# Unrolled head pairs in MLA, maxima finished in PSUM, and a new order within an attention step

## The reference

```python
for i in range(DEPTH):                       # kinds 0, 1, 2, 0
    hc = mod_norm(xc, norm_g[i], sh_c, sc_c) # 256 context rows
    hl = mod_norm(xl, norm_g[i], sh_l, sc_l) # 1024 latent rows
    ...                                      # q, k, v by projection, rotary on the latents
    s = q @ k.T * scale                      # latents: 512 cached + 1024 own keys; context: its 256 own
    p = softmax(s)                           # SWA: band mask, and a sink logit in the denominator
    o = p @ v
    x = x + gate * ((o * silu(g)) @ w_out[i])
```

## Time and profile before

| | us |
|---|---|
| median of 3 runs | 3929.22 (3926.41 to 3936.61) |
| the profiled execution, its own time | 3931.54 |
| its span | 3929.7 |
| PE busy | 3555.3 (90%) |
| DVE busy | 2518.0 (64%) |
| ACT busy | 2168.8 (55%) |
| POOL busy | 1187.7 (30%) |

### The profile page before, as it was taken

The page is one execution under the profiler, slowest core; times in us unless marked ns, Lnnn a source line. Parts: engine busy times, 40 slices in busy tenths (PEclk is TensorE's granted clock), DMA queues, the critical chain, the costliest instruction groups (busy, mean ns, idle before and its releaser), DMA issues. The chain is left out here.

```text
span 3929.7 us, 83391 instructions
## 1 busy us (share of the span) xinstructions
PE 3555.3 (90%) x33644; PEld 2063.9 (53%) x33644; DVE 2518.0 (64%) x3616; ACT 2168.8 (55%) x2859; POOL 1187.7 (30%) x851
## 2 busy tenths in 40 slices
PE   6999888889999988888899998888999989888898
PEld 3554555555455555555545555665455445455554
DVE  6335767767457468888845528998443567677754
ACT  5433766667434357777733226777233457667661
POOL 0000344445220024444421004555110014444442
PEclk9999999999999999999999999999999999899999
DMA  6237423232112342222111335442112562222111
GB/s 248 63 99 224 98 60 76 59 70 60 64 37 73 118 115 61 66 61 62 44 68 39 97 119 126 93 93 63 63 48 71 170 169 44 47 47 51 40 48 61
DMA packets 373325, 325.63 MB, mean 83 GB/s; under 512 B 246272, under 2 KB 294080, under 8 KB 371424
## 3 DMA queue, kind: packets, MB, share of 16 engines
q1 hardware_dynamic: 372960, 320.24, 30.0%
HBM read 228.94 MB, written 91.23 MB: 81 GB/s over the span
## 5 line engine op out<-in xcount | busy, mean ns | idle before, releaser
L2058 DVE TENSOR_REDUCE max_parts<-bank 128x1 f32<-128x512 f32 (+2 forms) x1536 | 974.3, 649 | 431.6 <-PE bank L2003 414.6
L2235 PE MATMUL bank<-q_slots,k_slots 96*128 96x512 f16 (+7 forms) x3968 | 1082.1, 375 | 78.3 <-issue 54.0
L2414 POOL TENSOR_TENSOR p_lo<-p_f,p_hi 128x1024 f16<-128x1024 f32 x352 | 787.5, 2237 | 1058.3 <-ACT p_hi L2316 985.2
L2308 ACT ACTIVATE p_f<-bank 128x1024 f32<-128x1024 f32 (+2 forms) x768 | 742.4, 967 | 581.6 <-PE bank L2235 475.0
L798 PE MATMUL bank<-H_hilo,w_hilo 128*128 128x512 f16 (+1 forms) x5760 | 1046.3, 344 | 13.9 <-DVE w_hilo L1048 8.8
L798 PEld LDWEIGHTS bank<-H_hilo,w_hilo 128*128 128x128 f16 x5760 | 563.8, 98 | 496.2 <-DVE w_hilo L1048 9.9
L2316 ACT ACTIVATE p_hi<-bank 128x1024 f16<-128x1024 f32 (+2 forms) x768 | 739.4, 963 | 0.0
L2003 PE MATMUL bank<-k_slots,q_slots 96*128 96x512 f16 (+4 forms) x1536 | 578.6, 378 | 102.9 <-ACT q_slots L2084 83.5
L2235 PEld LDWEIGHTS bank<-q_slots,k_slots 96*128 96x128 f16 (+2 forms) x3968 | 355.5, 100 | 353.9 <-issue 131.0
L2364 DVE TENSOR_TENSOR p_lo<-p_f,p_hi 128x1024 f16<-128x1024 f32 (+1 forms) x416 | 494.6, 1189 | 36.1 <-ACT p_hi L2316 35.5
L2209 PE MATMUL bank<-cq_hilo,p_hi 128*128 128x65 f16 x3200 | 339.8, 194 | 9.4 <-POOL p_lo L2414 5.8
(11 more groups left out here) (206 smaller groups left out, 4113.1 us busy)
## 6 DMA issues: line engine op xcount, KB each, us to landing
ada_w<-in_w_ada SPq DMA_DIRECT2D x48, 768.0 KB, 6.2
gate<-z_ring SPq DMA_DIRECT2D x32, 640.0 KB, 3.2
gate_rows<-gate SPq DMA_DIRECT2D x32, 640.0 KB, 4.2
q_slots<-q_mla SPq DMA_DIRECT2D x64, 240.0 KB, 3.2
k_mla<-H_hilo SPq DMA_DIRECT2D x64, 224.0 KB, 3.2
k_slots<-k_mla SPq DMA_DIRECT2D x64, 224.0 KB, 4.6
cq_hilo<-v_scratch SPq DMA_DIRECT2D x64, 224.0 KB, 4.1
v_lo_hi_one<-v_scratch SPq DMA_DIRECT2D x64, 224.0 KB, 4.3
```

Of the source, the lines that this page charges most:

```text
L2058: dve.tensor_reduce(mx[:, o, t, c:c + 1], entry_bank(i, b, n)[:, 0:nk], AX.X, ALU.max).then_inc(s_red.h, 1)
L2235: scored = pe.matmul(dst, lhs, rhs, start=(m == 0), stop=(m == len(ops) - 1), skip_group_check=swa)
L2308: act.activation(p32[:, p % 2, 0:cols], src, ACT.Exp, scale=scale).then_inc(s_p32.h, 1)
L2414: pool.tensor_tensor(pl[:, slot[p], 0:cols], p32[:, p % 2, 0:cols], ph[:, slot[p], 0:cols], ALU.subtract).then_inc(s_pp.h, 1)
```

## The change

It has six parts, all in `attention`.
1. `pairs_of_heads` writes out the eight pairs in MLA too; the loop is gone on all five engines.
2. The joined maxima go to the first columns of the PSUM bank of the unit's last `max` entry, and `neg_max` is computed from there. The tile `max_rows` is gone. PE's ring waits for such an entry now ask for `neg_max` to be written.
3. The lists are new. A `turn` is the first entry of its step, ACT copies its row before `p_f` and not after `p_hi`, c0 and c1 are a step earlier, and turn 0 is a step later in MLA and GQA.
4. DVE takes one entry, then makes `p_lo`, and then takes the second entry.
5. `p_f` has three buffers in place of two, and `p_hi` and `p_lo` use four slots everywhere. Before it was three slots for the first 18 steps of a pair and four for the last 8 in MLA and GQA, and three in SWA. The value product stays two steps behind.
6. In SWA the sink is added to the denominator by POOL (`add_sink`) and no longer by DVE. `norm` stands ahead of `p_lo` in POOL's order.

```diff
-        m4 = sb("max_rows", [P, 3, 4], F32)
...
-        out_step = [{3: 1, 4: 2}, {8: 0}] if swa else [{5: 1, 6: 2}, {10: 0}]
+        out_step = [{4: 1, 5: 2}, {8: 0}] if swa else [{5: 1, 6: 2}, {11: 0}]
...
         if swa:
-            own = [b_[4:6], b_[6:8] + c_[:1], c_[1:] + [turn(1)], [turn(2)], [], [], [], [], []]
-            ahead = [[], [], a_[:1], a_[1:2], a_[2:4], a_[4:7], a_[7:] + b_[:1], [turn(0)] + b_[1:3], mod + b_[3:4]]
+            own = [b_[4:6] + c_[:1], c_[1:] + b_[6:7], [turn(2)] + b_[7:], [turn(1)], [], [], [], [], []]
+            ahead = [[], [], [], a_[:2], a_[2:4], a_[4:6], a_[6:], b_[:3], [turn(0)] + b_[3:4] + mod]
         else:
-            own = [b_[5:7], b_[7:9] + c_[:1], c_[1:] + b_[9:11], b_[11:] + [turn(2)], [turn(1)]] + [[]] * 8
-            ahead = [[]] * 4 + [a_[:2], a_[2:4], a_[4:6], a_[6:8], a_[8:10], a_[10:] + b_[:1], mod + b_[1:2],
-                                [turn(0)] + b_[2:3], b_[3:5]]
+            own = [b_[5:7] + c_[:1], c_[1:] + b_[7:9], b_[9:11], [turn(2)] + b_[11:], [turn(1)]] + [[]] * 8
+            ahead = [[]] * 4 + [a_[:2], a_[2:4], a_[4:6], a_[6:8], a_[8:10], a_[10:], b_[:2], mod + b_[2:3],
+                                [turn(0)] + b_[3:5]]
...
-        slot = [p % 3 for p in range(P2 - 4 * fours)] + [p % 4 for p in range(4 * fours)]
+        LAG = 2
+        def slot(i, p):
+            return (i * P2 + p) % 4
...
         def pairs_of_heads(eng, body):
-            if mla:
-                peeled(eng, NB, body)
-            else:
-                for i in range(NB):
-                    body(i, i == 0, i == NB - 1)
+            for i in range(NB):
+                body(i, i == 0, i == NB - 1)
...
-                dve.tensor_reduce(m4[:, o, 0:nt], mx[:, o, 0:nt, 0:parts[u]], AX.X, ALU.max).then_inc(s_m4.h, 1)
+            dve.tensor_reduce(mb[:, 0:nt], mx[:, o, 0:nt, 0:parts[u]], AX.X, ALU.max).then_inc(s_m4.h, 1)
...
-                    dve.tensor_scalar(negm[:, par, 0:nt], m4[:, o, 0:nt], -1.0 / MAX_UNIT, None, ALU.mult
-                                      ).then_inc(s_neg.h, 1)
+                dve.tensor_scalar(negm[:, par, 0:nt], mb[:, 0:nt], -1.0 / MAX_UNIT, None, ALU.mult
+                                  ).then_inc(s_neg.h, 1)
...
-        p32 = sb("p_f32", [P, 2, 1024], F32)
+        p32 = sb("p_f32", [P, 3, 1024], F32)
...
+                            for k in items(b, p % NS, last):
+                                copy_rows(act, i, b, k)
                             act.wait_ge(s_sc.h, s_sc.base + g + 1)
-                            if above_zero(g - 1):
-                                wait_lo(act, i, p - 2)
-                            act.activation(p32[:, p % 2, 0:cols], src, ACT.Exp, scale=scale).then_inc(s_p32.h, 1)
+                            if above_zero(g - 2):
+                                wait_lo(act, i, p - 3)
+                            act.activation(p32[:, g % 3, 0:cols], src, ACT.Exp, scale=scale).then_inc(s_p32.h, 1)
...
-                            for k in items(b, p % NS, last):
-                                copy_rows(act, i, b, k)
...
-                        dve.wait_ge(s_es.h, s_es.base + hd * 3 + turn_order[u] + 1)
-                        dve.tensor_tensor(rd[:, un % 2, 0:nt], den, es32[:, hd % 3, u, 0:nt], ALU.add
-                                          ).then_inc(s_den.h, 1)
...
-                        for k in found[:2]:
+                        for k in found[:1]:
                             take_entry(dve, i, b, k)
                         ...                       # p_lo of step p - 1, if it is DVE's
+                        for k in found[1:2]:
+                            take_entry(dve, i, b, k)
                         inverse(i, p, first)
...
+                def add_sink(i, un):
+                    if not swa:
+                        return
+                    ...
+                    pool.tensor_tensor(den, den, es32[:, hd % 3, u, 0:nt], ALU.add).then_inc(s_den.h, 1)
...
+                            for u in range(3):
+                                done = last_of[u] + LAG
+                                un = 3 * b + u - 3 * (done // NS)
+                                if done % NS == j and (i or un >= 0):
+                                    add_sink(i, un)
+                                un = 3 * b + u - 3 * ((done + 1) // NS)
+                                if (done + 1) % NS == j and (i or un >= 0):
+                                    norm(i, un)
                             if j in pooled:
                                 p_lo(i, b * NS + j)
-                            if j in (1, 2) and not (first and b == 0):
-                                norm(i, 3 * b - 3 + j)
-                            if j == last_of[0] + 3:
-                                norm(i, 3 * b)
```

More of the change, by code:

```diff
@@ L1788, in attention @@
         count = lambda k, which: sum(e[0] in which for e in order[:k])
-        nmax = [count(k, ("max",)) for k in range(NE + 1)]
+        last_max = [e for u in range(3) for e in maxima_of(u)[-1:]]
+        nmax = [sum(e[0] == "max" and e not in last_max for e in order[:k]) for k in range(NE + 1)]
         nturn = [count(k, ("turn",)) for k in range(NE + 1)]
@@ L1916, in wait_bank @@
                 earlier = [m for m in range(n) if stream[b][m][0] == 1]
-                if len(earlier) >= 2:
-                    wait_taken(pe, i, b, earlier[-2])
+                for m in earlier[-2::-2]:
+                    if wait_taken(pe, i, b, m):
+                        return
                 return
@@ L1925, in wait_bank @@
                 if isinstance(i, int) and i < 0:
-                    pe.wait_ge(s_red.h, s_red.base + sum(e[0] == "max" for e in before_all))
+                    pe.wait_ge(s_red.h, s_red.base + nmax[len(before_all)])
+                    pe.wait_ge(s_neg.h, s_neg.base + 1)
                     pe.wait_ge(s_mr.h, s_mr.base + sum(e[0] == "turn" for e in before_all))
@@ L2057, in take_entry @@
                 dve.wait_ge(s_nz.h, s_nz.base + 1)
[L2058 to L2070 removed]
+            mb = entry_bank(i, b, n)
+            found = dve.tensor_reduce(mx[:, o, t, c:c + 1], mb[:, 0:nk], AX.X, ALU.max)
+            if e not in last_max:
+                found.then_inc(s_red.h, 1)
+                return
+            found.then_inc(s_m4.h, 1)
+            dve.wait_ge(s_red.h, s_red.base + hd * NM + nmax[k])
+            dve.wait_ge(s_m4.h, s_m4.base + hd * 6 + 2 * o + 1)
+            dve.tensor_reduce(mb[:, 0:nt], mx[:, o, 0:nt, 0:parts[u]], AX.X, ALU.max).then_inc(s_m4.h, 1)
+            dve.wait_ge(s_m4.h, s_m4.base + hd * 6 + 2 * o + 2)
+            if swa:
+                if above_zero(hd * 3 + o - 1):
+                    dve.wait_ge(s_es.h, s_es.base + hd * 3 + o - 1)
+                dve.tensor_scalar(negm[:, par, 0:nt], mb[:, 0:nt], sink_raw[:, at(hd)], -1.0 / MAX_UNIT,
+                                  ALU.max, ALU.mult).then_inc(s_neg.h, 1)
+            else:
+                dve.tensor_scalar(negm[:, par, 0:nt], mb[:, 0:nt], -1.0 / MAX_UNIT, None, ALU.mult
+                                  ).then_inc(s_neg.h, 1)
         def copy_rows(act, i, b, n):
@@ L2218, in body @@
                 def body(i, first, last):
-                    for p in range(P2 + 2):
+                    for p in range(P2 + LAG):
                         if p < P2:
@@ L2247, in body @@
                                 emit_entry(pe, i, b, k)
-                        if (p >= 2 or not first) and (p < P2 or last):
-                            pv(i, p - 2)
+                        if (p >= LAG or not first) and (p < P2 or last):
+                            pv(i, p - LAG)
                         if p < P2:
@@ L2296, in body @@
                 def body(i, first, last):
-                    for p in range(P2 + (2 if last else 0)):
+                    for p in range(P2 + (LAG if last else 0)):
                         if p < P2:
@@ L2430, in body @@
                     if last:
-                        norm(i, 4)
-                        norm(i, 5)
+                        for un in (4, 5):
+                            add_sink(i, un)
+                            norm(i, un)
                         split_out(pool, i, 1)
```

55 lines of the change are left out of this document (30 added, 25 removed).

## The result

The changed kernel takes 3734.05 us (median of 4 runs, 3727.24 to 3736.31) for 3930.26 us before. The ratio is 0.9496, with a 95% interval of 0.9479 to 0.9514: 196 us or 5.0% faster. The forecast was 3713 us, in a range of 3650 to 3805 us. The profiled execution took 3734.57 us, with a span of 3732.8 us.

The account below looks back on a forecast made before the run. PE was taken to bound the kernel, with 321 us of room from idle time and low clock in attention. Terms of -85, -37, -58 and -36 us gave -216 us: 3715.5 us, as a median 3713 us, range 3650 to 3805 us.

Parts of the forecast that it names:

- the likeliest case: Whole kernel: all terms come as forecast, -216 us, a median of 3713 us; chance 0.48.
- The loop, -85 us: MLA, layers 0 and 3: without the loop the step back, its wait and the low clock go, 40 and 45 us.
- MLA besides, -37 us: MLA: its share of term 2, PE's waits for ACT's copy of the turned row overtaken, -37 us.
- term 2: MLA and GQA: turns and ACT's copy first remove PE's ring waits, -57 us (37 in MLA, 20 in GQA).
- GQA, -58 us: GQA: early copy -20, DVE's `p_lo` wait -25, clock -18, price at turn 1 net +5 us.
- the price at turn 1: The last maximum behind DVE's `p_lo` stalls PE: +16 us, net +5, in GQA; no stall in MLA.
- rival E: GQA and SWA: POOL's late `p_lo` still collides with DVE's; 155 us gained, 3774 us; chance 0.15.
- E's sign: DVE: `p_lo` of 2 to 3 us would show rival E, that the collision stays.
- SWA, -36 us: SWA: sink moved to POOL and shorter `neg_max` relieve DVE, PE's `neg_max` wait goes, -36 us (0 to 58).
- terms 2 to 5: Turns and copy first; DVE's second place with `neg_max` from PSUM; third `p_f` and fourth slot (no gain); sink on POOL.

Follow-up runs that it names:

- e1: The kernel before with the pairs of MLA written out and nothing else changed: 3842.8 us.
- e7: e1 with `neg_max` computed from PSUM; lists, orders, buffers and sink as in the kernel before: 3763.0 us.
- e6: The changed kernel with DVE taking two entries ahead of `p_lo` again: 3682.3 us.
- e3: The changed kernel with, in SWA, `norm` behind `p_lo` and the previous pair's two output splits two steps later in POOL's order: 3701.5 us.
- e9: The changed kernel with the sink in SWA added by DVE again: 3738.1 us.
- e4: The changed kernel with the joined maxima back in SBUF, so `neg_max` is computed from there: 3900.4 us.

## Why the prediction was right, and where it wasn't

The direction, the range and the likeliest case were right: 196 us for 216 us. Part of that agreement is luck, since a term that was too large and terms that were too small made up for each other. The runs split the way from e1 to the changed kernel into three steps (differences of the periods times 16, in us, minus is faster; MLA is both layers):

| step | MLA | GQA | SWA |
|---|---|---|---|
| `neg_max` from PSUM (e1 to e7) | -20 | -57 | +1 |
| lists, early copy, buffers, sink (e7 to e6) | -42 | -24 | -15 |
| DVE's second place (e6 to the changed kernel) | +24 | +9 | +21 |

By the terms of the prediction:

1. **The loop, -85 us.** e1 gave 83 to 87 us. The reading of the "issue" waits and of the heads with and without a step back was right, also in that written-out code runs without such waits.
2. **MLA besides, -37 us.** From e1 to the changed kernel the two MLA layers fell by 1.24 and 1.09 us a head, times 16 that is 37 us. That the sum is met exactly is luck. PSUM made 20 us of it (e7: 0.64 and 0.59 us a head), where the prediction put nothing, because PE showed hardly a wait for DVE there. The lists and the early copy gave 42 us, near the 37 us of term 2 (and 24 us in GQA for its 20), so that term was read well. DVE's second place took 24 us back, where the prediction saw no stall.
3. **GQA, -58 us.** It was 64 us over 15 periods. The collision at 3.15 us was read rightly, but the prediction gave the cure to two parts together. e7 shows that PSUM alone ends it, and e6 that `p_lo` in second place costs 0.6 us a head in GQA. The mis-sized term is the price at turn 1: it was put at net +5 us in GQA and nothing in MLA. The wait was 13.6 us in GQA, near the 16 us forecast, but 9.9 and 9.7 us in MLA, where the estimate had the result 0.1 us early. The estimate counted 1.22 us for DVE's `p_lo` of step 2, and the runs show 1.7 to 2.16 us. That is the mechanism of rival E: `norm` first, POOL's `p_lo` late, DVE's `p_lo` held up. It came in GQA and in MLA too, where E did not look. It was cheaper than E had it, because PE no longer waits for that `p_lo` but only for the maximum behind it, and for POOL's own `p_lo` (17.0 us in GQA, 6.0 before). So E's sign, a `p_lo` of 2 to 3 us on DVE, was seen, and E's time was not.
4. **SWA, -36 us.** It was nothing, and this is the step that failed: "3 additions of at most 1.67 us fit in". It counted POOL's free time over the stretch and not its place in the order. POOL had the time, but `norm` and the splits now stood ahead of a `p_lo` that PE waits for. With that order mended alone SWA falls by 2.4 us a head (e3), 36 us over 15 periods and 33 us in the median, about the size of the term. The wait of 11.8 us for `neg_max` was forecast to go and is 12.0 us: `neg_max` itself fell to 0.22 us, but in the new lists its maximum and turn 1 stand one step later, and DVE's second place (21 us in the table) puts that maximum behind `p_lo`. DVE is busy for 270 us where about 250 was expected, 14 us of it because its `p_lo` is held up by POOL more than before. The additions themselves were harmless: 46 of the 48 took 0.2 us, and e9 is no faster or slower.

The range given as "from half to the full size of terms 2 to 5" should read 3713 to 3779 us by the prediction's own sum, and not 3680 to 3760; the measured time lies in both. The 11.2 us before turns in GQA left out a second wait there, 4.3 us for `neg_max`, so the net was -2 us and not +5.

The total alone would have hidden this. Of the 196 us, the loop and one operand make 167 us (e7). The four other parts make 29 us together: the lists, the early copy, the buffers and the sink, 81 us (e6 against e7), stand there against DVE's second place, 52 us. In SWA POOL's order hides another 33 us.

## What to carry to other kernels

An operation of a few columns on the way to the bound engine can cost more than a large one: look for its longest instance and not its mean, and for what another engine was reading then. When the order within a step is changed, follow the last entry of each chain to the instruction that waits for it; here a wait of 45 us cost 59 us. An edit taken back from the new kernel says what it is worth to the new order, and not what it gained over the old one. A share of free time says that work fits in, and only the order says whether it fits before what is waited for.

## What the runs showed of the hardware

- A step back of the hardware loop cost 8.3 to 9.4 us with all that follows from it, for a bare wait of 5 to 6 us (before and e1).
- A DVE `tensor_scalar` of 128 x 4 with its operand in SBUF took 1.89 us in the mean over layer 3 of e4, where it falls under a GpSimd operation that reads SBUF in nearly every head, and 0.16 us from PSUM in the changed kernel.
- It works both ways: a GpSimd subtraction of 128 x 512 took 2.18 us under a DVE `p_lo` (the SWA head above), and 1.15 us where it ran before DVE's `p_lo` began (e4, layer 3):

```profile
3502.07 1.15 POOL L1985 TENSOR_TENSOR H_hilo<-ckv_hilo,H_hilo 128x512 f16<-128x512 f32 x1
```
